# A two-layer decoder trunk: modulation tiles split around the first norm, and expert rows gathered by indirect DMA

## The reference, cut to what matters

```python
def block(x, c, pos, p, cache):
    mod = (silu(c) @ p['w_ada'] + p['b_ada'])[:, None, :]       # c: 9 rows; w_ada: 1024 x 6144
    shift1, scale1, gate1, shift2, scale2, gate2 = split(mod, 6, axis=-1)
    h = rmsnorm(x, p['g_norm1']) * (1.0 + scale1) + shift1
    mixed, new_state = token_mixing(h, pos, p, cache)           # one input projection, four mixers
    x = x + gate1 * mixed
    h = rmsnorm(x, p['g_norm2']) * (1.0 + scale2) + shift2
    x = x + gate2 * hier_moe(h, ...)    # top-1 of 4 groups, then top-2 of 8 SwiGLU experts in it
    return x, new_state
```

## Time and profile before

| | us |
|---|---|
| median of 3 runs (lowest to highest) | 2448.66 (2439.2 to 2452.95) |
| the profiled execution | 2429.46 |
| its span on the core | 2427.7 |
| PE busy (matmul) | 1864.5 |
| DVE busy | 677.6 |
| ACT busy | 307.3 |
| POOL busy | 169.1 |

### The profile page before, as it was taken

How to read it: one execution, slowest core, us unless ns; L and a number is a source line. 1 busy time by engine, 2 the same in 40 slices (tenths; PEclk the granted TensorE clock), 3 DMA queues, 4 the chain that set the end, 5 groups by cost and what they waited for, 6 DMA issues and landing times.

```text
span 2427.7 us, 22046 instructions
## 1 busy us (share of the span) xinstructions
PE 1864.5 (77%) x8727; PEld 939.4 (39%) x8727; DVE 677.6 (28%) x1388; ACT 307.3 (13%) x555; POOL 169.1 (7%) x203
## 2 busy tenths in 40 slices
PE   5699365556689999999777955546577899999993
PEld 2366253223533333333335644412244333333332
DVE  1221534332322222222203143532333222222212
ACT  1122200121011000000011130011200000000001
POOL 1000011421000000000000010133300000000000
PEclk9799655767779999999978985567686999999997
DMA  9621101887109999999990201058930699999990
GB/s 360 271 85 54 62 14 45 299 313 290 70 3 420 421 421 421 421 422 420 376 417 36 87 23 56 14 197 321 355 141 0 252 421 421 421 421 421 421 405 22
DMA packets 97209, 609.51 MB, mean 251 GB/s; under 512 B 12475, under 2 KB 12739, under 8 KB 39632
## 3 DMA queue, kind: packets, MB, share of 16 engines
q1 hardware_dynamic: 82944, 562.07, 56.9%
q0 software_dynamic: 14160, 46.00, 5.5%
HBM read 602.21 MB, written 5.81 MB: 250 GB/s over the span
## 4 chain that ended last, share of the span: by engine, by line
PE 56%; DMA 22%; DVE 13%; ACT 5%; issue 2%; POOL 1%; POOLq 0%; SPq 0%; PEldq 0%; DVEq 0%; ACTq 0%; PEld 0%
DMA ring<-in_w_gate 15%; PE PS L1024 15%; PE PS L625 9%; PE PS L1047 7%; DVE big L1460 4%; DMA ring<-in_w_ada 4%; PE PS L1005 3%; PE PS L959 3%; PE PS L547 3%; PE PS L905 2%; DVE mT L1460 2%; PE PS L842 2%; DMA ring<-in_sb_kv,idxu 2%; ACT big L1183 1%; DVE big L1466 1%
## 5 line engine op out<-in xcount | busy, mean ns | idle before, releaser
L1024 PE MATMUL PS<-ring,big 128*64 128x512 f32 x2048 | 486.0, 599 | 19.2 <-issue 12.5
L1024 PEld LDWEIGHTS PS<-ring,big 128*64 128x64 f32 x2048 | 163.6, 138 | 320.9 <-issue 280.1
L547 PE MATMUL PS<-cst,big 128*128 128x128 f32 (+5 forms) x557 | 106.3, 330 | 228.6 <-ACT big L1183 84.9
L1460 DVE TENSOR_TENSOR big<-big,PS 128x320 f32<-128x320 f32 (+4 forms) x278 | 138.3, 498 | 511.1 <-PE PS L1047 503.7
L1074 PE MATMUL PS<-ring,big 128*64 128x512 f32 x1024 | 228.4, 597 | 8.5 <-ACT big L1187 8.5
L1187 ACT ACTIVATE big<-PS 128x512 f32<-128x512 f32 (+7 forms) x165 | 91.8, 562 | 986.8 <-PE PS L547 570.7
L625 PE MATMUL PS<-mT,ring 128*128 128x320 f32 x768 | 213.5, 439 | 2.0 <-PE PS L625 1.9
L547 PEld LDWEIGHTS PS<-cst,big 128*128 128x128 f32 (+5 forms) x557 | 74.1, 165 | 299.9 <-DVE big L1460 107.0
L1047 PE MATMUL PS<-rv,mT 128*128 128x320 f32 x512 | 172.2, 459 | 6.3 <-ACT mT L1187 2.4
L625 PEld LDWEIGHTS PS<-mT,ring 128*128 128x128 f32 x768 | 146.8, 192 | 67.2 <-issue 8.0
L2090 POOL DMA_INDIRECT ring<-in_sb_kv,idxu x128 | 122.7, 958 | 205.5 <-PE PS L905 162.5
(11 more groups left out here) (285 smaller groups left out, 1433.7 us busy)
## 6 DMA issues: line engine op xcount, KB each, us to landing
ring<-in_w_gate SPq DMA_DIRECT2D x128, 1024.0 KB, 11.3
ring<-in_w_up SPq DMA_DIRECT2D x128, 1024.0 KB, 11.9
ring<-in_w_down SPq DMA_DIRECT2D x128, 1024.0 KB, 14.6
ring<-in_w_ada SPq DMA_DIRECT2D x24, 2048.0 KB, 15.8
ring<-in_sb_kv SPq DMA_DIRECT2D x128, 256.0 KB, 5.5
ring<-in_w_in SPq DMA_DIRECT2D x12, 2048.0 KB, 16.1
ring<-in_win_kT SPq DMA_DIRECT2D x8, 2048.0 KB, 8.8
ring<-in_win_v SPq DMA_DIRECT2D x8, 2048.0 KB, 10.4
```

Source lines behind the costliest of these rows:

```text
L547: return nc.tensor.transpose(out, in_, ident[0:in_.shape[0], 0:in_.shape[0]])
L1024: i = mm(PS[SLOTS * x:SLOTS * x + SLOTS, bank, :], M.rows[:, p % 4, k, x * SLOTS:(x + 1) * SLOTS], half3(h, 4)[:, k % 4, :], start=(k == 0 ...
L1460: return V.tensor_tensor(out, a, b, op)
```

## The change: what it does

In stage_a only 8 of the 12 `w_ada` tiles come ahead of the projection. PE forms the rows of tiles 0 to 3 (shift1, scale1), then the sum of squares, then the transposes of the small vectors, then turns tiles 0 to 3; DVE scales x by the reciprocal root meanwhile and finishes the norm when the four tiles are turned. Tiles 4 to 7 follow on PE, each row product, ACT copy and turn in sequence, before PE waits for `h_done`. Tiles 8 to 11 go behind `w_in` in SP's order (ring positions 14 to 17: slots 2, 3, 0, 1) and are consumed by PE at the head of stage_gla, ahead of the GLA scores.

In stage_out the transposes of `mT` move up, to right behind the router product; ACT's three copies of them stand before `pair_exps` in its order. POOL writes the token-major rows to a DRAM tensor. The product `gather()` is gone: PE multiplies `pick` by a column of token numbers (15 products of one column), DVE casts the 640 numbers to integers, and POOL issues five indirect DMAs that fetch 128 rows of 4 KB each. At the head of the experts stage PE turns chunks 0 and 1 of the sorted rows, ACT copies them, and DVE cuts the first window; chunks 2 and 3 are turned between gate and up of pair 0, chunk 4 after up. The windows have two buffers in place of four.

```diff
 # SP
-                for j in range(12):
+                for j in range(8):
                     load(w_ada[l, j:j + 1], j % RING, base + j // RING)
                 for j in range(6):
                     load(w_in[l, j:j + 1], (IN0 + j) % RING, base + (IN0 + j) // RING)
+                for j in range(8, 12):
+                    load(w_ada[l, j:j + 1], ada_at(j) % RING, base + ada_at(j) // RING)
 # PE, stage_a
+                for j in range(4):
+                    mod_rows(l, j, 3 + j)
+                rms()
                 pe.wait_ge(loads, l * LOADS + LOADS_PRE + LOADS_A)
 ...
-                pe.wait_ge(sem["vec_T"], 1)
-                pe.wait_ge(sem["mod_done"], 1)
-                rms()
+                for j in range(4):
+                    i = mod_turn(j + 1, j % 4, 0, j % 4)
+                i.then_inc(sem["mod_mm"], 1)
+                for j in range(4, 8):
+                    mod_rows(l, j, 3 + (j - 4) % 3)
+                    i = mod_turn(j + 1, j % 4, 6, j % 4)
+                i.then_inc(sem["mod_mm"], 1)
                 pe.wait_ge(sem["h_done"], 1)
 # PE, stage_gla
+                for j in range(8, 12):
+                    mod_rows(l, j, 4 + j % 3 if j < 11 else 4 + 8 % 3)
+                    if j > 8:
+                        mod_turn(j - 8, (j - 9) % 2, 7, j - 9)
+                mod_turn(4, 1, 7, 3).then_inc(sem["mod_mm"], 1)
                 pe.wait_ge(sem["gla_operands"], 1)
 # PE, stage_out: the 3 x 8 transposes of mT now stand right behind router_mm, and
-                gather()
                 pe.wait_ge(sem["picks"], 1)
+                for c in range(ROWS // 128):
+                    for t, (t0, w) in enumerate(SPANS):
+                        i = mm(PS[:, 7, c:c + 1], moe.pick[0:w, t, c * 128:(c + 1) * 128], K("token")[0:w, t:t + 1], start=(t == 0), stop=(t == 2))
+                i.then_inc(sem["slots_mm"], 1)
 # ACT, stage_out
-                act.wait_ge(sem["pair_args"], 1)
-                f(moe.dx, moe.dx, ACT.Exp).then_inc(sem["pair_exps"], 1)
                 for t, (t0, n) in enumerate(SPANS):
                     act.wait_ge(sem["rows_turned"], t + 1)
                     copy(moe.htok[0:n, t, :]...).then_inc(sem["rows_kept"], 1)
+                act.wait_ge(sem["pair_args"], 1)
+                f(moe.dx, moe.dx, ACT.Exp).then_inc(sem["pair_exps"], 1)
 # POOL, new
+            def stage_out(l):
+                for t, (t0, n) in enumerate(SPANS):
+                    pool.wait_ge(sem["rows_kept"], t + 1)
+                    dma(h_rows[l][t0:t0 + n], moe.htok[0:n, t, :], rows_written)
+                pool.wait_ge(sem["slots_kept"], 1)
+                pool.wait_ge(rows_written, 48 * (l + 1))
+                for c in range(ROWS // 128):
+                    pool.indirect_dma_start(out=moe.staged[c], out_offset=None, in_=h_rows[l],
+                                            in_offset=bass.IndirectOffsetOnAxis(ap=slot_token[:, c:c + 1], axis=0)).then_inc(sorted_full[c], 16)
 # PE, experts
+                turn_sorted(0)
+                turn_sorted(1)
                 for p in range(PAIRS):
                     gate(p)
+                    if p == 0:
+                        turn_sorted(2)
+                        turn_sorted(3)
                     if p:
                         slot_sums(p - 1, range(8))
                     up(p)
+                    if p == 0:
+                        turn_sorted(4)
 # DVE, window(p)
+                dve.wait_ge(sem["sorted_kept"], min(max(p, 1) + 1, 5))
```

More of the change, by code:

```diff
@@ L371, in trunk @@
             hsel = L3(10880, 8, ROWS + SLOTS)
-            rows = v4(big, 5888, 4, 8, 128)
+            rows = v4(big, 5888, 2, 8, 128)
+            staged = [big[:, 5888 + 1024 * c:6912 + 1024 * c] for c in range(4)] + [vAC[:, 0:1024]]
             wpick = v4(big, 9984, 2, 3, 128)
@@ L1287, in stage_b, with stage_gla @@
                 copy(mT[:, 4:6, 0:256], PS[:, 6:8, 0:256])
-            def stage_gla():
+            def stage_gla(l):
                 G = gla
+                for j in range(8, 12):
+                    keep_mod_rows(l, j, j % 2, 4 + j % 3 if j < 11 else 4 + 8 % 3)
                 rsqrt(G.sq)
@@ L1503, in norm @@
                 c(tt(mT, xT, spread(rr[:, :], 1, KT8), M_))
+            def norm(g, shift, scaled=False):
+                sc = v3(scaleT_, 0, 8, 9)
+                c(tt(sc, modT[:, shift + 8:shift + 16, :], spread(vec[:, g:g + 8], 2, 9), M_))
+                if not scaled:
+                    scale_x()
                 hp = mT[:, :, 0:SEQ]
@@ L2010, in _ @@
                 with dve.If(many > 0):
+                    for full in sorted_full:
+                        dve.wait_ge(full, 16 * (l + 1))
                     with dve.Fori(0, NE // 4) as it:
@@ L2105, in _ @@
                     barrier_lead(pool)
+                stage_out(l)
                 barrier_lead(pool)
```

158 lines of the change are left out of this document (84 added, 74 removed).

## The result

The changed kernel takes 2324.99 us (median of 4 runs, 2320.4 to 2329.22); beside it the kernel before took 2443.93 (2435.45 to 2452.95). The ratio is 0.9512, 95% interval 0.9466 to 0.9558: faster, by 119 us.

The account below looks back on a forecast made before the run. Bound by a serial line of twelve tiles then the norm in stage_a, and by the DMA stream in the experts. Terms -72 (stage_a), -36 (stage_out), +15 (stage_gla) give -93 us: 2356 us, range 2328 to 2395.

Parts of the forecast that it names:

- Stage_a: Both layers' stage_a: norm hidden behind serial tiles on PE, small projections earlier; 72 us won, 54 to 81.
- the tile: Each serial tile 4 to 7 in stage_a: 3.65 us at the high clock, 6.2 at the low, 4.7 taken.
- Stage_gla: Head of stage_gla: GLA scores wait for late tiles 10 and 11; 7.5 us a layer, 15 lost, 9 to 25.
- rival D: Stage_gla: tiles 10 and 11 land late, state load beside them; 12.6 us a layer, -83, 2366 us; chance 0.05.
- Stage_out and experts: One-hot gather replaced by indirect DMAs, less a loss in pair 0; 17.8 us a layer, 36 won, 24 to 47.
- The way from pick to gate: Stage_out into experts: 46.4 us removed, replaced by products, cast, indirect DMAs, barrier, turns, copy and window in line, 21.4.
- Landing "taken as nothing": Stage_out's gathers land within the time they have; no cost, up to 6 us if they take twice as long.
- Pair 0: First expert pair: chunks 2 and 3 between gate and up delay SP's second four halves; 3 us lost, 0 to 9.
- From the profile to the median: Whole kernel: the profile's 93 us gain taken from the median 2448.66, 19 above the profiled execution, giving 2356 us.
- A: Clock stays low in stage_a's serial tiles; stage_a wins 54, stage_gla loses 18: -72, 2377 us; chance 0.17.
- B: Expert stage gives the gain back, stage_out wins only 9 a layer: -75, 2374 us; chance 0.12.
- C: Expert stage stays at the low clock, 27 us more a pair; 2518 us with three pairs a layer; chance 0.05.

Follow-up runs that it names:

- norm-only run: Kernel before with only the change to stage_a and stage_gla, the one-hot gather kept; 2364.8 us against 2444.9, ratio 0.9692.
- the nine traces with the same code: Kept traces, of several kernels, whose code for tiles 4 to 7 is the changed kernel's: 18 passes, 72 tiles, 17 of them slow.
- the repeat: The changed kernel run once more, unedited; 2323.6 us (2320.1 to 2327.2), profiled execution 2320.1.
- the run with the spread tiles: Changed kernel with tile 10's rows behind the GLA scores, tile 11's behind the state products, their turns at stage_gla's end; 2319.6 us.
- the second trace of before: Kernel before run once more, unedited, with its own profile; 2441.5 us over 10 runs, span 2441.0 where the first trace had 2427.7.
- the run with the three repairs: Changed kernel with the exponential behind the first copy, GLA state loaded a stage earlier, tiles 10 and 11 spread over stage_gla; 2291.1 us.

## Why the prediction was right in its mechanism and wrong in its time

*Stage_a, 72 us forecast, 85.8 measured (40.9 + 44.9).* The mechanism is as forecast: no transfer on the path behind tile 3, the norm done at 64.2 us behind the tiles, serial tiles on PE. The mis-sized term is **the tile, 4.7 us forecast, 3.63 measured in seven of eight and 5.1 in the other**: 7.1 us of the 13.8, 4.3 in layer 0 and 2.8 in layer 1. I had the high-clock sum, 3.65, right to 0.02 us and the low one, 6.2, as well (6.17 in the norm-only run), and took a value between them for all. That seven of eight sat at the fast end is in part luck of this trace: over the nine traces with the same code the tile took 4.0 us on average, and in layer 0 of the norm-only run 5.25. The reason given, that the tiles begin behind unbroken work, fails: the low level came in the middle of such work. The neighbours that I carried over at their old lengths came out shorter too, by another 8.2 us in the two layers: the sum of squares to the next product 4.41 us in place of 6.62, five transposes 0.53 in place of 1.2, and the small projections to the input projection 10.6 and 10.4 in place of 11.8 and 11.6. One step cost more: tile 3's rows end at 45.7, not 42.5, since it came 1.8 us later and ran at 1.2 GHz after 4.80 us of waiting. In layer 1 the first four tiles don't wait, and took 8.7 us for 9.4 forecast. The forecast's fast end, 39.6 and 41.1 us, left the shorter neighbours out, so even it was too slow.

*Stage_gla, 15 us lost forecast, 14.2 measured from the projection to stage_out.* The place is right: scores 20.7 us behind the stage's start, 19.0 in layer 1, some 17 forecast. The size is near in part by luck. Stage_gla itself lost 7.7 and 4.2 us for 7.5 each; the other stages of these rows, which vary by 2 to 4 us, make it 3.5 and 10.7, and 7.0 and 8.4 in the repeat. The GLA state's landing stands beside the tiles at full height, which only rival D named, in half a sentence: the run with the spread tiles shows it as the next wait, 8.57 us.

*Stage_out and experts, 36 us forecast, 38.9 measured.* The way from pick to gate was forecast at 21.4 and is 20.7 in layer 0. Its parts partly cancel: the 15 products take 7.33 us and not 5.6, at a granted clock of 0.50 (window of 641 to 662); from DVE's cast (its end at 648.66) to PE's first turn it is 6.3 us for 8.2 allowed (4.8 + 3.4). The exponential behind the third copy costs 4.0 (4.2 forecast). Landing "taken as nothing" holds in layer 0 and costs 2.96 us in layer 1; the existing loads that it was measured by do not fetch beside a full stream, as I had it, but beside 168 to 367 GB/s (before, windows of 30 us from 410 to 590). Pair 0 gives back 1.2 and 0.9 us, not 3: SP's second batch comes 8.9 us behind the first, not 10.8, and the first keeps the engines busy for 10.

*From the profile to the median.* **This step failed too, and it is the one that put the time outside the range**: "the median of the runs shown, 2448.66, is 19 above that execution; the same 93 from it gives 2356". The changed kernel's median is 4.6 us above its profiled execution. So the miss of 31 us is 16 in the sum (109.1 against 93) and 14.6 here. The 109.1 lies inside the forecast's own ends of 53 to 119, and taken from 2448.66 it would have given 2339.6, inside the range. The offset was not a constant of the measurement, and 2448.66, a median of three runs, itself lay above the later medians of before (2440.9 to 2444.9). In the second trace of before, 9.8 of the 13.3 us by which it is longer lie in the one-hot gather, at a lower granted clock; this is the work that the change takes out, and its length went with it. The runs without a trace fit this: the two kernels that keep the one-hot gather spread most, before from 2430 to 2470 us over the three comparisons and the norm-only kernel from 2362.9 to 2393.0, while all others spread by 2 to 16, the changed kernel by 9. Which stretch varied in them is not shown.

*The rivals.* A, the low clock in serial tiles, was met in one tile of eight in the changed kernel, and in three of four in layer 0 of the norm-only run; it fails as a mechanism, since in every pass that began with slow tiles the later ones came back to the high level within the loop. The Trainium skill, page "TensorE: Matmul & The Clock Gate", section "HAM oscillation", describes bursts of products parted by waits for transfers that are longer than the burst, behind each of which the next burst starts cold. This case's traces agree where PE had idled 4.8 to 9.9 us: the tile behind it took 3.2 to 3.6 us. The waits of 0.7 us inside the tiles are shorter than the products between them and not that section's case. B and C are refuted by the window of the experts, 421 GB/s at clock 1.00, and by gate(0) to the last `down`, which is within 1.2 us of before. D did not come in size: it had 25 us for stage_gla, and 14.2 were lost, though its state load beside the tiles was there.

What stays open: why the same tiles got 0.50 in layer 0 of the norm-only run, from the middle of unbroken products on, and 0.99 in layer 0 of the changed kernel; and why the first tile of layer 1 is slow in eight of nine traces with no idle time ahead of it. The idle time before tile 3 does not decide it: 4.80 us in the changed kernel, with no slow tile behind, and 4.78 in the run with the three repairs, with two.

## What to carry to other kernels

Where a stretch of small products runs at either of two clock levels, forecast the two times with a chance each, and look at a second trace of the kernel before carrying an offset from one execution to a median: the part that you remove may be the part that varies. Late transfers moved into a later stage collide with what that stage loads; two waits of equal length side by side hide each other, and only the repair of both shows their price. Read a repair in its own stage as well as in the median: the spread tiles won 12.9 us there, and the median showed 4.

## What the runs showed of the hardware

After 9.13 and 9.94 us of idle time the first tile took 3.24 and 3.64 us, and the next ran at 1.92. In layer 0 of the norm-only run three tiles were slow before the fourth ran at 1.92. In the one-hot gather, 96 records without a gap that begin at 1.2 GHz, the level rose some 15 us behind the start in one execution and some 25 in another of the same kernel. The five indirect DMAs of 128 rows of 4 KB were issued 1.25 us apart (0.95 busy and 0.30 between) and landed in 4.4 to 8.2 us; their median of 5.8 is that of the existing indirect loads, 5.7, which are half as large but land beside transfers of 168 to 367 GB/s. A 256 KB load issued beside two 2 MB tiles landed in 9.8 us, in 4.8 in the kernel before, and in 3.7 one stage earlier.
